# A two-block transformer kernel on one core: the first norm's operand taken from a transposed copy of x

## The reference, cut to what matters

```python
h = x                                              # x: (1, 256, 1024) float32
y = xf * lax.rsqrt(jnp.mean(xf * xf, axis=-1, keepdims=True) + EPS) * g     # rmsnorm
proj = rmsnorm(h, g_norm) @ w_in                   # w_in: 1024 x 6144
q, k, v, gate = jnp.split(proj, [1024, 2048, 4096], axis=-1)
q = rotary(heads(q, 256), pos)                     # k the same, and scaled
```

## Time and profile before

| | us |
|---|---|
| device time, median of 3 runs (lowest, highest) | 866.22 (866.06, 866.31) |
| span of the profiled execution (first to last instruction) | 864.7 |
| PE busy in it | 856.5 (99%) |
| DVE busy | 604.2 (70%) |
| ACT busy | 501.3 (58%) |
| moved from HBM | 152.53 MB |

### The profile page before, as it was taken

How to read it: one execution, slowest core, us unless ns; L and a number is a source line. 1 busy time by engine, 2 the same in 40 slices (tenths; PEclk the granted TensorE clock), 3 DMA queues, 4 the chain that set the end, 5 groups by cost and what they waited for, 6 DMA issues and landing times.

```text
span 864.7 us, 12203 instructions
## 1 busy us (share of the span) xinstructions
PE 856.5 (99%) x4654; PEld 733.2 (85%) x4654; DVE 604.2 (70%) x1068; ACT 501.3 (58%) x873; POOL 36.1 (4%) x49
## 2 busy tenths in 40 slices
PE   9999999999999999999999999999999999999996
PEld 8998888888889999978888788888888888888885
DVE  6986666655767885779687466788458566777584
ACT  6435545446655676968678457654535456766540
POOL 0000000000010000000000001100020000000002
PEclk9999999999999999999999999999999999999999
DMA  9864544652583877543332457573764555434421
GB/s 326 280 222 166 195 149 144 207 194 98 195 268 128 285 241 233 148 147 98 127 119 97 146 194 225 191 269 126 265 202 153 182 195 192 150 120 172 165 79 49
DMA packets 86808, 154.36 MB, mean 179 GB/s; under 512 B 3744, under 2 KB 24352, under 8 KB 86752
## 3 DMA queue, kind: packets, MB, share of 16 engines
q1 hardware_dynamic: 85248, 149.19, 51.3%
q0 software_dynamic: 1360, 4.33, 1.7%
q10 hardware_dynamic: 144, 0.07, 0.0%
HBM read 152.53 MB, written 1.05 MB: 178 GB/s over the span
## 4 chain that ended last, share of the span: by engine, by line
PE 97%; DVE 1%; DMA 0%; ACT 0%; POOL 0%; issue 0%; DVEq 0%; POOLq 0%
PE acc L2273 11%; PE acc L2275 11%; PE acc L2274 11%; PE acc L2247 9%; PE acc L2249 9%; PE acc L2248 9%; PE acc L2291 5%; PE acc L2285 4%; PE acc L2286 4%; PE acc L2287 4%; PE acc L2292 3%; PE misc L2315 2%; PE misc L2445 2%; PE misc L2434 1%; PE acc L2305 1%; PE misc L2487 1%
## 5 line engine op out<-in xcount | busy, mean ns | idle before, releaser
L1455 DVE TENSOR_TENSOR wboth<-raw,wboth 128x1024 fp32r<-128x1024 f32 (+1 forms) x280 | 326.4, 1214 | 60.5 <-ACT wboth L973 59.0
L973 ACT ACTIVATE wboth<-raw 128x1024 fp32r<-128x1024 f32 (+1 forms) x280 | 278.9, 1052 | 122.9 <-PE acc L2275 67.4
L2273 PE MATMUL acc<-wboth,xhiA 128*128 128x512 f32 x272 | 107.8, 396 | 0.0
L2275 PE MATMUL acc<-wboth,xloA 128*128 128x512 f32 x272 | 106.1, 390 | 0.0
L2274 PE MATMUL acc<-wboth,xhiA 128*128 128x512 f32 x272 | 106.1, 390 | 0.0
L2247 PE MATMUL acc<-wboth,xhiA 128*128 128x512 f32 x240 | 93.9, 391 | 0.0
L2249 PE MATMUL acc<-wboth,xloA 128*128 128x512 f32 x240 | 93.5, 390 | 0.0
L2248 PE MATMUL acc<-wboth,xhiA 128*128 128x512 f32 x240 | 93.4, 389 | 0.0
L2291 PE MATMUL acc<-xC,wboth 128*128 128x512 f32 x192 | 68.7, 399 | 0.0
L2273 PEld LDWEIGHTS acc<-wboth,xhiA 128*128 128x128 f32 x272 | 51.1, 188 | 11.4 <-issue 1.2
L2275 PEld LDWEIGHTS acc<-wboth,xloA 128*128 128x128 f32 x272 | 51.0, 188 | 10.9
(11 more groups left out here) (335 smaller groups left out, 1721.0 us busy)
## 6 DMA issues: line engine op xcount, KB each, us to landing
raw<-in_w_in_dram SPq DMA_DIRECT2D x36, 1024.0 KB, 5.2
raw<-in_ret_w_in_dram SPq DMA_DIRECT2D x22, 1024.0 KB, 5.6
raw<-in_nsa_w_in_dram SPq DMA_DIRECT2D x16, 1024.0 KB, 5.5
raw<-in_kv_w_dram SPq DMA_DIRECT2D x12, 1024.0 KB, 6.7
raw<-in_ret_w_out_dram SPq DMA_DIRECT2D x8, 1024.0 KB, 5.1
raw<-in_ple_w_gate_dram SPq DMA_DIRECT2D x8, 1024.0 KB, 5.1
raw<-in_nsa_w_out_dram SPq DMA_DIRECT2D x8, 1024.0 KB, 5.1
raw<-in_cmp_w_k_dram SPq DMA_DIRECT2D x4, 1024.0 KB, 5.5
```

Source lines behind the costliest of these rows:

```text
L973: nc.scalar.activation(to_hi, src, ACT.Copy).then_inc(hi_done, 1)
L1455: nc.vector.tensor_tensor(to_lo, src, to_hi.bitcast(F32), ALU.subtract).then_inc(lo_done, 1)
L2273: nc.tensor.matmul(o, xh, hi[:, j, off:off + cols], start=start, stop=False)
L2275: ins = nc.tensor.matmul(o, xl, hi[:, j, off:off + cols], start=False, stop=stop)
```

## The change

x is handed in a second time, transposed on the host to 128 x 8 x 256 (`x_T`), and loaded into a free region of SBUF in four parts (block 0; block 1; blocks 2 and 3; blocks 4 to 7). ACT issues parts 0, 2 and 3, SP part 1. The gain's 8 columns are loaded by themselves, ahead of the identity, which ACT issues last. The 16 transposes are gone, and ACT and DVE split each block from SBUF. The rows of x are loaded by SP behind chunk 5. ACT sums the squares behind the split of chunk 5, all four in a row, and DVE adds them behind its chunk 5. "roots" stands behind the whole of chunk 5 in PE's order.

```diff
+XT_CUTS = (0, 1, 2, 4, 8)
@@ tensor_order
-    norm("ret")
     r("ret_q0")
-    plan.half("ret_k0", 0, 0)
+    r("ret_k0", [0])
     m("roots")
-    plan.half("ret_k0", 0, 1)
     r("ret_k0", [1])
@@
+        def xT_part(i):
+            return x_T[:, XT_CUTS[i]:XT_CUTS[i + 1]], w["x_T"][:, XT_CUTS[i]:XT_CUTS[i + 1]]
+
+        def xT_wait(eng, k):
+            if k in XT_CUTS:
+                eng.wait_ge(xT_in[XT_CUTS.index(k)], 16)
@@ sync
-            for m in range(MT):
-                sp.dma_start(h[:, m], w["x"][0, m * P:m * P + P]).then_inc(x_in[m], 16)
             for c, (key, src, ks, width, *_) in enumerate(plan.chunks):
...
+                if c == 0:
+                    sp.dma_start(*xT_part(1)).then_inc(xT_in[1], 16)
                 if c == 5:
+                    for m in range(MT):
+                        sp.dma_start(h[:, m], w["x"][0, m * P:m * P + P]).then_inc(x_in[m], 16)
@@ scalar, first_norm_hi
+                act.wait_ge(ret_gain_in, 16)
                 for k in range(KD):
-                    misc_wait(act, "norm", "ret", k % 4)
-                    if k >= 4:
-                        act.wait_ge(operand_ready, xt_no["norm", "ret", k - 4] + 1)
-                    nc.scalar.activation(xhi["A"][:, k], first_columns(k), ACT.Copy, scale=cv["ret"][:, k:k + 1])
+                    xT_wait(act, k)
+                    nc.scalar.activation(xhi["A"][:, k], x_T[:, k], ACT.Copy, scale=cv["ret"][:, k:k + 1])
@@ scalar
-            act.dma_start(head[:], w["head"]).then_inc(head_in, 16)
+            act.dma_start(*xT_part(0)).then_inc(xT_in[0], 16)
+            act.dma_start(head[:, P:], w["head"][:, P:]).then_inc(ret_gain_in, 16)
             act.wait_ge(warm_set, 1)
             nc.scalar.activation(ssq[:, 0, 0:1], gains[:, 0, 0:1], ACT.Copy)
-            act.wait_ge(head_in, 16)
+            act.dma_start(*xT_part(2)).then_inc(xT_in[2], 16)
+            act.dma_start(*xT_part(3)).then_inc(xT_in[3], 16)
+            act.dma_start(head[:, 0:P], w["head"][:, 0:P]).then_inc(head_in, 16)
             first_norm_hi()
+            split_until(len(FIRST_CUTS))
             for m in range(MT):
                 act.wait_ge(x_in[m], 16)
                 for nb in range(2):
                     square(m, nb)
-                split_until(len(FIRST_CUTS) + m)
+            split_until(len(FIRST_CUTS) + 1)
@@ vector
-                        out=xlo["A"][:, k], in0=first_columns(k),
+                        out=xlo["A"][:, k], in0=x_T[:, k],
@@
             first_norm_lo()
+            split_until(len(FIRST_CUTS))
             norm_stats("ret", 0)
-            split_until(len(FIRST_CUTS))
             asked = norm_stats("ret", 1)
             dve.wait_ge(*asked)
+            dve.wait_ge(head_in, 16)
@@ tensor
-                            pe.wait_ge(head_in, 16)
-                            for m, ks in ((0, (0, 4, 1, 5, 2)), (1, (0, 4)), (0, (6, 3, 7)), (1, (1, 5, 2, 6, 3, 7))):
...
-                                    ins = nc.tensor.transpose(first_columns(k)[:, m * P:m * P + P],
-                                                              h[:, m, k * P:k * P + P], ident)
...
                 elif kind == "roots":
+                    pe.wait_ge(head_in, 16)
                     pe.wait_ge(roots_spread, 1)
```

More of the change, by code:

```diff
@@ L577, in build @@
         ret_kT = k3("ret_kT", 2048, 8)
-        here[0] += 2048
+        x_T = k3("x_T", 2048, KD)
         sTd = [carve(f"sTd{i}", 384) for i in range(2)]
@@ L673, in build @@
         head_in = sem("head_in")
+        ret_gain_in = sem("ret_gain_in")
+        xT_in = [sem(f"xT_in{i}") for i in range(len(XT_CUTS) - 1)]
         trig_in = sem("trig_in")
@@ L809, in build @@
         ones = gains[:, 0, 0:P]
-        def first_columns(k):
-            at_ = k // 4 * T
-            return bank("norm", "ret", k % 4)[:, at_:at_ + T]
+        def xT_part(i):
[3 more added lines that the diff above has]
+                eng.wait_ge(xT_in[XT_CUTS.index(k)], 16)
         def scores_of(hd, mp, qt):
@@ L1004, in first_norm_hi @@
             def first_norm_hi():
+                act.wait_ge(ret_gain_in, 16)
                 for k in range(KD):
-                    misc_wait(act, "norm", "ret", k % 4)
-                    if k >= 4:
-                        act.wait_ge(operand_ready, xt_no["norm", "ret", k - 4] + 1)
-                    nc.scalar.activation(xhi["A"][:, k], first_columns(k), ACT.Copy, scale=cv["ret"][:, k:k + 1])                        .then_inc(operand_hi_done, 1)
+                    xT_wait(act, k)
+                    nc.scalar.activation(xhi["A"][:, k], x_T[:, k], ACT.Copy, scale=cv["ret"][:, k:k + 1])\
+                        .then_inc(operand_hi_done, 1)
                     xts[0] += 1
@@ L1501, in first_norm_lo @@
                     dve.wait_ge(operand_hi_done, xts[0])
-                    freed[("norm", "ret", k % 4)] = xt_on(nc.vector.scalar_tensor_tensor(
-                        out=xlo["A"][:, k], in0=first_columns(k),
+                    xt_on(nc.vector.scalar_tensor_tensor(
+                        out=xlo["A"][:, k], in0=x_T[:, k],
                         scalar=cv["ret"][:, k:k + 1], in1=xhi["A"][:, k].bitcast(F32), op0=ALU.mult, op1=ALU.subtract))
@@ L2327, in misc @@
                     j = name[2]
-                    if name[1] == "ret":
-                        if j == 0:
-                            pe.wait_ge(head_in, 16)
-                            for m, ks in ((0, (0, 4, 1, 5, 2)), (1, (0, 4)), (0, (6, 3, 7)), (1, (1, 5, 2, 6, 3, 7))):
-                                pe.wait_ge(x_in[m], 16)
-                                for k in ks:
-                                    ins = nc.tensor.transpose(first_columns(k)[:, m * P:m * P + P],
-                                                              h[:, m, k * P:k * P + P], ident)
-                                    if m and k >= 4:
-                                        ins.then_inc(misc_full[k % 4], 1)
-                        return
-                    else:
[L2340 to L2347, removed]
+                    if name[1] == "kv":
+                        m, k0 = divmod(KD // 2 * j, KD)
+                        pe.wait_ge(rows_normed, m + 1)
+                        parts = [(xn_kv[:, m, k * P:k * P + P], P) for k in range(k0, k0 + KD // 2)]
+                    else:
+                        pe.wait_ge(residual_piece, 4 * (NORMS.index(name[1]) - 1) + MT * (1 + j // 2))
+                        parts = [(h[:, m, k * P:k * P + P], P) for k in (2 * j, 2 * j + 1) for m in range(MT)]
+                    ins = transposes(ps, parts)
                 elif kind == "roots":
+                    pe.wait_ge(head_in, 16)
                     pe.wait_ge(roots_spread, 1)
@@ L2564 @@
         [tables[k] for k in CONST_ORDER] + [columns(_np.asarray(cols[k])) for k in COLUMNS], axis=1)))
+    args["x_T"] = give("x_T", _np.ascontiguousarray(
+        _np.asarray(inputs["x"])[0].reshape(T, KD, P).transpose(2, 1, 0)))
     rows = _np.concatenate([_np.asarray(inputs["p"])[:, 0], _np.asarray(inputs["p_2"])[:, 0]], axis=0)
```

## The result

The changed kernel takes 869.15 us as the median of 11 runs (867.94 to 869.77), the kernel before, run beside it on the same chip, 866.31 (11 runs, 866.06 to 867.70). The ratio is 1.0029 with a 95% interval of 1.002 to 1.0037: it is slower by 2.8 us, where 0.7 was forecast, and outside the range of 865.4 to 868.1. The changed kernel's runs lie 1.8 us apart, those of before 0.53 but for one.

The account below looks back on a forecast made before the run. PE bounds the kernel, with 97% of the chain of waits. Span 864.7 - 0.35 (start) + 1.1 (wait at ret_q1) = 865.4, with 1.5 outside it 866.9 us, +0.7 on the median 866.22; range 865.4 to 868.1.

Parts of the forecast that it names:

- Chunk 2 takes most of that back: At the start: chunk 2 lands at 9.1 us, leaving only about 0.5 of the 2.1 us gained.
- The start: Everything up to PE's k = 2 matmuls together: a gain of 0.35 us, bounds -0.6 and +2.1.
- The first matmul: PE's first matmul of ret_q0 comes at 6.0 us instead of 8.09, 2.1 us earlier.
- TensorE's rate: Opening matmuls: PE's idle time may delay its step from 1.2 to 2.4 GHz; start gain 0.5, 0.1 or -0.6 us.
- rival (a): At the start: the lower PE rate lasts to about 12 us, start -0.6, total 867.9 us; chance 0.17.
- Rows of x and squares, moved: Behind chunk 5: later x and squares stay hidden, 4 us to spare; chunk 6 lands about 21, 2 us to spare.
- Roots, moved: At ret_q1: with roots behind all of chunk 5, PE waits 1.1 us for DVE, bounds 0 and 2.
- (b): At the start: chunk 2 passes part 3 and lands at 7.6, total 865.3 us; chance 0.13.
- (c): At ret_q1: no wait, DVE being quicker than counted, total 865.9 us; chance 0.06 alone, 0.04 with (b).
- (d): New loads don't open earlier: gain lands after 6, or x or chunk 6 late; 868 us and more; chance 0.08.
- Splitting from SBUF: ACT's and DVE's block splits, from SBUF instead of PSUM: no cost counted, bounds 0.05 us a block either way.

Follow-up runs that it names:

- e2: The changed kernel with the roots back in the middle of chunk 5, nothing else: 867.74 us, ratio 1.0017 to the kernel before.
- i1: The changed kernel with the roots back in the middle of chunk 5 and eight products of ones instead of four: 867.30 us.
- i2: i1 with each of the four parts of x_T contiguous in HBM: 866.78 us.
- g1: f1 with eight products of ones instead of four: 866.53 us.
- f1: The changed kernel with the roots back in the middle of chunk 5 and x_T in one transfer, first on SP's queue: 868.09 us.
- g4: The changed kernel with six products of ones instead of four, nothing else: 868.94 us.
- e4: The changed kernel with each part of x_T contiguous in HBM, same queues and order: 868.42 us.
- f2: f1 with x_T taken from an array laid out so that its rows are 1 KB: 868.34 us.
- f3: The changed kernel, roots in the middle of chunk 5, x_T in two halves on SP's queue, ahead of chunk 0 and behind chunk 2: 866.98 us.
- e3: The kernel before with only the roots moved behind the whole of chunk 5: 867.53 us.
- h1: The kernel before with x loaded in eight transfers of 32 whole rows each instead of two transfers: 869.42 us.
- h3: g3 with DVE making only the first half of chunk 7's low part before it rotates ret_q0: 865.90 us.
- g2: f3 with eight products of ones instead of four: 867.16 us.
- g3: f1 with the identity and gain in one transfer and eight products of ones instead of four: 866.45 us.

## Why the prediction was wrong

**The account.** From the changed kernel back to the kernel before: roots back, 869.15 to 867.74 (e2), 1.41; products of ones, to 867.30 (i1), 0.44; contiguous parts, to 866.78 (i2), 0.52; one transfer on one queue, to 866.53 (g1), 0.25; the rest to 866.31 to 866.41, about 0.2. The steps are not independent (products of ones give 1.56 from f1 to g1 and 0.44 from e2 to i1), so their sizes hold for this order. The 0.44 is not clear of the scatter: the runs of e2 and i1 overlap (867.03 to 868.75 and 867.11 to 868.11). By the medians, the loads are thus 0.77 of the loss (i1 to g1) and the roots 1.2 to 1.4; what the rest, 0.7 to 0.8, is made of isn't shown.

**The step that failed** is "Chunk 2 takes most of that back": it "lands at 8.9 as before, or 0.1 to 0.3 later", "1.05 + 0.07 + 1.05 MB again, at the same 377 GB/s". It landed at 11.4. In the three other profiles with these loads it landed at 11.2, 10.2 and 9.5, later than the upper bound of 9.2 each time. Both factors were wrong. 377 GB/s was read in the window of 8 to 20 us, and over 2 to 7 us the engines delivered 250 here (332 in the kernel before); that parts cut out of 8 KB rows lower it, i1 and i2 show. And 2.17 MB counted only what had been issued ahead, where 2.95 MB had moved by then; in the kernel before it was 2.39 as well, so both could have been checked against windows of its start. The start was put at a gain of 0.35 (bounds -0.6 to +2.1); in the profile it was a loss of 1.93. The text named the test, "wrong ... if chunk 2 lands ... after 10", and that is what came.

**The first matmul**, forecast at 6.0: 6.36, behind a gain that landed at 5.3 instead of 4.95. Right in kind. ACT's later issues "from 3.05 to 4.25" was wrong: they stood at 1.72 to 3.08, beside the table load. This brought parts 2 and 3 and the identity forward, beside chunks 1 and 2. That it is a source of the bytes beside chunk 2 was not tested by itself.

**TensorE's rate**, rival (a). In the changed kernel's profile the upper rate held from the first matmul on, so the term was zero there. In e2, g4, e4, f1, f2 and f3 the lower rate came, with idle time of PE ahead of it. What it cost differs: from f1 to g1 it is 1.56 us; in g4's profile 1.4; in e2's, whose start is the changed kernel's own, nothing, since chunk 2 came later still. Between the profiles of e2 and i1 ret_k0 moves by 1.78 us (21.41 to 19.63), and ACT's start on chunk 2 by 1.79 (11.27 to 9.48). So the scatter of the changed kernel's runs fits landings that vary; a part for the clock is possible (g4) and not shown.

**Rows of x and squares, moved: hidden.** For the roots it was right: squares done at 21.9, diagonal at 23.2 instead of 21.1, wanted at 27.4. Chunk 6, "about 21", landed at 22.8, and in the profile PE didn't wait for it. But the text gave it 2 us to spare on PE's account alone. Where the start is repaired (g1), it is DVE that is late through it, in front of the tables, and this takes 0.33 of 0.54 us.

**Roots, moved: a new wait of 1.1 us.** Right, in place, releaser and size: 3.03 - 1.93 = 1.10 in the profile, 1.24 in e3, 1.41 in e2. The mechanism is shown from both sides.

**The other rivals.** (b), chunk 2 at 7.6, didn't happen: it landed behind part 3 (10.7) in the changed kernel, and at 9.5, just ahead of it (9.7), in i1. The Trainium skill ("DMA: Bandwidth & Descriptors", Queues, rings and completion order) has an engine drain a packet of typically 9 to 17 descriptors from one queue before it switches; with that chunk 2 could have passed, and no profile here has it landing by 8.0. (c) fell with the wait. (d), which was given 0.08, names the cause in the wrong place: the late loads were chunks 1 and 2, for which the text had no rival at all on the late side beyond 0.3 us.

**Splitting from SBUF** was put at nothing, bounds 0.05 us a block. ACT's first block took 0.51 against 0.47 us, DVE's 0.48 in both: right.

**Open.** Why the engines are slower on parts cut out of 8 KB rows, when the same bytes in one transfer with 1 KB rows (f2) go at 355 GB/s, and why they are slow on h1's contiguous blocks of 32 rows. And why the same loads gave 256, 283, 275 and 315 GB/s over 3 to 7 us, and landings of chunk 2 from 9.5 to 11.4, in the profiles of the changed kernel, e2, g4 and i1.

## What to carry to other kernels

At the start of a kernel a load's landing is not its bytes over the best rate of the trace: take the rate and the bytes moved until such a landing from the windows of the very microseconds in question, and keep a rival in which each is wrong. Take more than one profile before a landing is explained: here one and the same set of loads landed chunk 2 over a range of 1.9 us. Hand the first operands in so that each transfer is contiguous; one transfer on the queue of the loads that follow did no worse than any other way here. Work taken away at the front of PE leaves a hole that the clock may charge for, and a producer moved back in PE's order eats the slack of the chain behind it, which can be counted beforehand.

## What the runs showed of the hardware

- Four parts of 128 to 512 KB whose rows are cut out of 8 KB rows: 250, 267, 260 and 291 GB/s over 2 to 7 us (the changed kernel, e2, g4, i1); the same transfers contiguous: 307 and 328 (e4, i2).
- The same loads, issued at the same times: one 512 KB chunk landed 9.3, 9.1, 8.1 and 7.4 us after its issue in these four profiles.
- The granted clock can read 1.00 while matmuls stand 0.22 us apart: it does in f1 from 7.36 to 12.65, as for the products of ones in the kernel before; in f3, at the same distances, it reads 0.50 over 9 to 11.
- ACT issued a transfer at 1.72 while its table load ran from 1.66 to 2.94: issues are not held behind it.
- An issue on SP takes 0.45 us, so 128 KB in each allow 290 GB/s at most. But blocks of 32 rows of 4 KB also kept the engines busy for longer: SP's queue took 94.7% of their time for 0.88 MB in h1 and 94.8% for 1.41 MB in the kernel before, 3 to 7 us.
- Eight products of ones, the same 16 instructions, took 5.36 us in h3 and 6.66 in g2 and g3, so the same cover ends up to 1.3 us later in another execution.
